# One layer of a hybrid diffusion backbone on one core: where the result is normalised, and three orders on three engines

## The reference

```python
h_lat = modulate(rms_norm(x, norm_g[l, 0]), mod_lat[0], mod_lat[1])     # h_ctx alike
m_ctx, m_lat = hybrid_mixer(h_ctx, h_lat, ...)      # gated DeltaNet heads and Mamba-2 heads, both directions
x = x + mod_lat[2] * rms_norm(m_lat, norm_g[l, 1])
h_lat = modulate(rms_norm(x, norm_g[l, 2]), mod_lat[3], mod_lat[4])
y_lat = ec_moe(h_lat, router_w[l], exp_w_gate[l], exp_w_up[l], exp_w_down[l])
x = x + mod_lat[5] * rms_norm(y_lat, norm_g[l, 3])
```

```python
gate, idx = lax.top_k(jnp.swapaxes(aff, 1, 2), cap)                # cap = 128
hid = silu(xs @ w_gate) * (xs @ w_up)
ye = (hid @ w_down) * gate[..., None]
y = zeros.at[bidx, idx].add(ye)                                    # a token may have several experts, or none
```

## Time and profile before

| what | us |
| --- | --- |
| median of 3 runs | 1538.88 (1536.69 to 1540.21) |
| the profiled execution | 1535.95 |
| its span, first to last instruction | 1534.1 |
| TensorE (PE) busy | 1312.0, 86% |
| VectorE (DVE) busy | 763.1, 50% |
| ScalarE (ACT) busy | 476.5, 31% |
| GpSimd (POOL) busy | 210.5, 14% |

### The profile page before, as it was taken

How to read it: one execution, slowest core, us unless ns; L and a number is a source line. 1 busy time by engine, 2 the same in 40 slices (tenths; PEclk the granted TensorE clock), 3 DMA queues, 4 the chain that set the end, 5 groups by cost and what they waited for, 6 DMA issues and landing times.

```text
span 1534.1 us, 13869 instructions
## 1 busy us (share of the span) xinstructions
PE 1312.0 (86%) x5053; PEld 759.5 (50%) x5053; DVE 763.1 (50%) x1080; ACT 476.5 (31%) x1109; POOL 210.5 (14%) x186
## 2 busy tenths in 40 slices
PE   6898889993999999988899978999239999999990
PEld 1444445441554555578888864455114444444440
DVE  1248878788760666637777764554640100110015
ACT  1625434351111122346666642333101010101003
POOL 0003210120100000015444410000010101110100
PEclk9899999997899999989999988999559999999995
DMA  8514343343142110035665572341729999999836
GB/s 307 154 28 147 112 144 117 103 122 100 69 138 82 42 27 28 9 96 158 184 186 181 179 272 98 136 150 56 265 78 334 341 341 328 333 339 342 282 83 232
DMA packets 173402, 257.81 MB, mean 168 GB/s; under 512 B 48861, under 2 KB 91606, under 8 KB 173334
## 3 DMA queue, kind: packets, MB, share of 16 engines
q1 hardware_dynamic: 152438, 208.52, 40.6%
q0 software_dynamic: 11392, 41.95, 9.2%
q10 hardware_dynamic: 9504, 6.45, 1.3%
HBM read 212.38 MB, written 44.50 MB: 167 GB/s over the span
## 4 chain that ended last, share of the span: by engine, by line
PE 68%; DVE 13%; ACT 10%; DMA 5%; issue 2%; SPq 2%; ACTq 0%; POOLq 0%; DVEq 0%
PE ps L1600 27%; PE ps L1056 15%; PE ps L1075 7%; PE ps L375 5%; DMA arena<-zt_dram 2%; PE ps L1020 2%; DVE arena L648 2%; PE ps L1558 2%; PE ps L458 2%; DVE arena L1961 1%; PE ps L1582 1%; ACT arena L1736 1%; PE ps L1045 1%; ACT arena L512 1%; DMA arena<-ada_w 1%
## 5 line engine op out<-in xcount | busy, mean ns | idle before, releaser
L1600 PE MATMUL ps<-arena 128*128 128x512 f32 (+1 forms) x1120 | 444.8, 557 | 0.0
L1600 PEld LDWEIGHTS ps<-arena 128*128 128x128 f32 x1120 | 214.0, 193 | 217.7 <-issue 212.3
L1056 PE MATMUL ps<-arena 128*128 128x512 f32 x512 | 227.9, 598 | 1.4 <-ACT arena L1172 1.4
L1961 DVE SCALAR_TENSOR_TENSOR arena<-arena,taps 128x1024 f32<-128x1024 f32 x160 | 223.5, 1397 | 5.7
L375 PE MATMUL ps<-arena 128*128 128x128 f32 x1080 | 136.5, 282 | 26.5 <-DVE arena L602 16.4
L1056 PEld LDWEIGHTS ps<-arena 128*128 128x128 f32 x512 | 96.9, 192 | 117.5 <-issue 115.5
L375 PEld LDWEIGHTS ps<-arena 128*128 128x128 f32 x1080 | 130.4, 197 | 35.9 <-issue 24.5
L1315 DVE TENSOR_TENSOR arena<-arena,ps 128x512 f32<-128x512 f32 x16 | 11.0, 688 | 226.5 <-PE ps L1056 226.5
L1020 PE MATMUL ps<-arena 128*128 128x512 f32 x256 | 116.2, 609 | 4.6 <-ACT arena L1121 4.6
L1075 PE MATMUL ps<-arena 128*128 128x512 f32 x256 | 112.6, 593 | 1.2 <-DVE arena L1322 1.2
L1020 PEld LDWEIGHTS ps<-arena 128*128 128x128 f32 x256 | 48.5, 194 | 62.9 <-issue 56.2
(11 more groups left out here) (280 smaller groups left out, 1593.4 us busy)
## 6 DMA issues: line engine op xcount, KB each, us to landing
arena<-exp_w_gate SPq DMA_DIRECT2D x16, 2048.0 KB, 11.2
arena<-exp_w_up SPq DMA_DIRECT2D x16, 2048.0 KB, 9.2
arena<-exp_w_down SPq DMA_DIRECT2D x16, 2048.0 KB, 11.0
arena<-ada_w POOLq DMA_DIRECT2D x16, 1024.0 KB, 6.2
arena<-w_in SPq DMA_DIRECT2D x28, 512.0 KB, 3.9
arena<-ada_w SPq DMA_DIRECT2D x4, 2048.0 KB, 10.6
arena<-x SPq DMA_DIRECT2D x16, 512.0 KB, 9.4
arena<-g_dram SPq DMA_DIRECT2D x16, 512.0 KB, 4.7
```

Source lines behind the costliest of these rows:

```text
L1056: last = mm(ps[gu_bank[s] + j][:], xsT[s][:, k, :], ew[s][j][:, k, :], start=(k == 0), stop=(k == KD - 1))
L1600: last = mm(ps[3 * (m % 2) + gi][:, 0:w], wring[(m + 1) % NW][:, k, :], hT[:, k, o:o + w], start=(k == 0), stop=(k == KD - 1))
L1961: ins = v.scalar_tensor_tensor(accg, cin_l[ci % 2][:, j // 3:j // 3 + GR, j % 3:j % 3 + GW], tp[:, j:j + 1], accg, ALU.mult, ALU.add)
```

## The change

There are five edits.

1. ScalarE's exponential of the blocks moves from the front of stage 12 to the end of stage 13.
2. On VectorE, `scores` moves from the end of an iteration (for `nxt`) to the next iteration, right behind `rest` (for `own`).
3. On GpSimd, `query_e` moves ahead of `with_eg` and `decayed_hs`.
4. GpSimd also stores each tile of x2 to `out` during the merge.
5. The end is rebuilt. `y_dram` is loaded once the first 14 experts' scatters have landed, into the memory of x2. Six of its tiles are normalised beside the products of experts 14 and 15, two behind them, and GpSimd adds each to `out` by an accumulating DMA. The rows of the tokens of experts 14 and 15 are then redone: their y rows are gathered, the expert's own result is added, they are normalised again, x2's rows (gathered from `out` earlier) are added, and the rows overwrite those in `out`. Expert 14's result is still scattered into `y_dram`, since 15 may share its tokens; expert 15's is not.

```diff
# 1 (scalar)
-                if m == M_Z0:
+                take_tile(m)
+                take_jobs(m)
+                if m == M_Z0 + 1:
                     act.wait_ge(sem("blk_dve"), 1)
                     a(yo_f, yo_f, ACT.Exp).then_inc(sem("blk_exp"), 1)
-                take_tile(m)
-                take_jobs(m)
# 2 (dve_scan)
                 if own and own[1] > 0:
                     rest(own)
+                if lat(own):
+                    scores(own)
                 if own and two:
                     mask_dn(dve, two)
...
                 if nxt:
                     block_y(nxt)
-                if lat(nxt):
-                    scores(nxt)
# 3 (pool_scan)
+                if lat(nxt):
+                    query_e(nxt)
                 if nxt and nxt[1] > 0:
                     with_eg(nxt)
                 if own and 0 < own[1] < LAST:
                     decayed_hs(own)
-                if lat(nxt):
-                    query_e(nxt)
# 4 (pool_tail, merge)
                 pool.dma_start(h2_t[ORD[t]], h2[t % 2]).then_inc(sem(f"h2_out{t % 2}"), 16)
+                pool.dma_start(out_t[ORD[t]], x2[:, ORD[t], :]).then_inc(sem("x2_out"), 16)
# 5 sp_tail
-            sp_.wait_ge(sem("y_sc"), 16 * E_N)
-            sp_.wait_ge(sem("down"), E_N)
+            sp_.wait_ge(sem("y_sc"), 16 * EL)
+            sp_.wait_ge(sem("x2_out"), 16 * NL)
             for t in range(NL):
                 sp_.dma_start(yt[:, t, :], y_t[t]).then_inc(sem(f"tile_in{t // 2}"), 16)
...
# 5 act_tail: six roots ahead of the copy of expert 15's hidT, two behind it, then those of the rows
             for e in range(E_N + 1):
+                if e == E_N:
+                    for t in range(N_FIRST):
+                        tile_root(t)
...
+            for t in range(N_FIRST, NL):
+                tile_root(t)
+            for i in range(LE):
+                act.wait_ge(sem("rows"), i + 1)
+                root_of(NL + i, yr[i])
# 5 dve_tail
             for e in range(E_N + 1):
+                if e == E_N - 1:
+                    for t in range(3):
+                        scaled(t, yt[:, t, :]).then_inc(sem("fin"), 1)
...                                                  # the hidden product of e
+                if e == E_N - 1:
+                    for t in range(3, N_FIRST):
+                        scaled(t, yt[:, t, :]).then_inc(sem("fin"), 1)
-                if e >= 1:
+                if 1 <= e < E_N:
...                                                  # ye of e - 1
+            dve.wait_ge(sem("ye"), E_N - 1)
+            dve.wait_ge(sem(f"xs_in{EL % NX}"), 16 * (E_N // NX + 1))
+            v.tensor_tensor(yr[0], yr[0], ye[EL % 2], ALU.add).then_inc(sem("rows"), 1)
+            for t in range(N_FIRST, NL):
+                scaled(t, yt[:, t, :]).then_inc(sem("fin"), 1)
+            dve.wait_ge(sem("down"), E_N)
+            dve.wait_ge(sem(f"xs_in{EL % NX + 1}"), 16 * (E_N // NX + 1))
+            for h in range(2):
...
+                ins = v.scalar_tensor_tensor(yr[1][:, hs_], ps[4 + h][:], gateT[:, E_N - 1:E_N], yr[1][:, hs_], ALU.mult, ALU.add)
+            ins.then_inc(sem("rows"), 1)
+            for i in range(LE):
+                link(scaled(NL + i, yr[i]))
+                dve.wait_ge(sem(f"xs_in{EL % NX - 2 + i}"), 16 * (E_N // NX + 1))
+                v.tensor_tensor(yr[i], yr[i], x2r[i], ALU.add).then_inc(sem("fin"), 1)
# 5 pool_tail
+            def added(t):
+                pool.wait_ge(sem("fin"), t + 1)
+                pool.dma_start(out_t[t], yt[:, t, :], accum_op=ALU.add).then_inc(sem("out"), 16)
-            for e in range(E_N):
+            for e in range(E_N - 1):
...
+                if e == EL - 1:
+                    pool.wait_ge(sem("x2_out"), 16 * NL)
+                    for i in range(LE):
+                        rows_in(x2r[i], out_rows, EL + i, EL % NX - 2 + i)
+                if e == EL:
+                    pool.wait_ge(sem("y_sc"), 16 * e)
+                    rows_in(yr[0], y_dram, EL, EL % NX)
+                    for i in range(NL // 2):
+                        pool.wait_ge(sem(f"tile_in{i}"), 64)
+                    for i in range(3):
+                        pool.wait_ge(sem(f"xs_in{i}"), 16 * (E_N // NX + 1))
+                    for t in range(N_FIRST):
+                        added(t)
...                                                  # wait for ye of e, scatter it
+            pool.wait_ge(sem("y_sc"), 16 * (E_N - 1))
+            rows_in(yr[1], y_dram, E_N - 1, EL % NX + 1)
+            for t in range(N_FIRST, NL):
+                added(t)
+            pool.wait_ge(sem("out"), 16 * NL)
+            for i in range(LE):
+                pool.wait_ge(sem("fin"), NL + i + 1)
+                if i > 0:
+                    pool.wait_ge(sem("out_rows"), 16 * i)
+                p.indirect_dma_start(out_rows, ...idxT of expert EL + i..., yr[i], None).then_inc(sem("out_rows"), 16)
```

More of the change, by code:

```diff
@@ L886, in hybrid_block @@
         gu_bank = (2, 6)
-        yt = arena[:, 0:NL * D].rearrange("p (t n) -> p t n", t=NL)
+        LE = 2
+        EL = E_N - LE
+        yt = x2
+        x2r, yr = (xs[EL % NX - 2], xs[EL % NX - 1]), (xs[EL % NX], xs[EL % NX + 1])
+        assert NX == 4 and EL % NX == 2
+        N_FIRST = 6
         wo_k = w_out.rearrange("a (k p) n -> (a p) k n", p=P)
@@ L895, in hybrid_block @@
         out_t = out.rearrange("a (t p) d -> (a t) p d", p=P)
+        out_rows = out.rearrange("a t d -> (a t) d")
         ORD = [NL // 2 - 1 - t // 2 if t % 2 == 0 else NL // 2 + t // 2 for t in range(NL)]
@@ L959, in sp_tail @@
                 load_down(e)
-            sp_.wait_ge(sem("y_sc"), 16 * E_N)
-            sp_.wait_ge(sem("down"), E_N)
+            sp_.wait_ge(sem("y_sc"), 16 * EL)
+            sp_.wait_ge(sem("x2_out"), 16 * NL)
             for t in range(NL):
                 sp_.dma_start(yt[:, t, :], y_t[t]).then_inc(sem(f"tile_in{t // 2}"), 16)
-            for t in range(NL):
-                sp_.wait_ge(sem("fin"), t + 1)
-                sp_.dma_start(out_t[t], yt[:, t, :]).then_inc(sem("out"), 16)
             sp_.wait_ge(sem("out"), 16 * NL)
+            sp_.wait_ge(sem("out_rows"), 16 * LE)
         def pe_tail(pe):
@@ L1172, in xs_copy, with root_of, tile_root @@
                 a(xsT[e % 2][:, 4 * h:4 * h + 4, :], heads(ps[0][:]), ACT.Copy).then_inc(sem("xsT"), 1)
+            def root_of(i, src):
+                a(sqj, src, ACT.Square, accum_out=ssq[:, i:i + 1]).then_inc(sem("ysq"), 1)
+                act.wait_ge(sem("ysq"), 2 * i + 1)
+                a(rstd[:, i:i + 1], ssq[:, i:i + 1], ACT.Sqrt, scale=1.0 / D, bias=eps1[:]).then_inc(sem("ysq"), 1)
+            def tile_root(t):
+                act.wait_ge(sem(f"tile_in{t // 2}"), 64)
+                root_of(t, yt[:, t, :])
             xs_copy(0, 0)
@@ L1309, in dve_tail, with scaled @@
             dve.wait_ge(sem("route"), 5)
+            def scaled(i, src):
+                dve.wait_ge(sem("ysq"), 2 * i + 2)
+                link(v.reciprocal(rstd[:, i:i + 1], rstd[:, i:i + 1]))
+                return v.scalar_tensor_tensor(src, src, rstd[:, i:i + 1], row5, ALU.mult, ALU.mult)
             for e in range(E_N + 1):
+                if e == E_N - 1:
+                    for t in range(3):
+                        scaled(t, yt[:, t, :]).then_inc(sem("fin"), 1)
                 if e < E_N:
@@ L1322, in dve_tail @@
                     v.tensor_scalar(ye[s][:, 512:D], ps[5][:], gateT[:, e - 1:e], None, ALU.mult).then_inc(sem("ye"), 1)
[L1323 to L1327, removed]
+            dve.wait_ge(sem("ye"), E_N - 1)
[6 more added lines that the diff above has]
+            for h in range(2):
+                hs_ = slice(h * 512, (h + 1) * 512)
+                ins = v.scalar_tensor_tensor(yr[1][:, hs_], ps[4 + h][:], gateT[:, E_N - 1:E_N], yr[1][:, hs_], ALU.mult, ALU.add)
[4 more added lines that the diff above has]
+                v.tensor_tensor(yr[i], yr[i], x2r[i], ALU.add).then_inc(sem("fin"), 1)
         def pool_tail(pool):
@@ L1345, in pool_tail, with rows_in @@
                 gather(e)
-            for e in range(E_N):
+            def rows_in(dst, src, e, k):
+                pool.wait_ge(sem("xsps"), 2 * (E_N - NX + k + 1))
+                p.indirect_dma_start(dst, None, src, bass.IndirectOffsetOnAxis(ap=idxT[:, e:e + 1], axis=0))\
+                    .then_inc(sem(f"xs_in{k}"), 16)
+            def added(t):
+                pool.wait_ge(sem("fin"), t + 1)
+                pool.dma_start(out_t[t], yt[:, t, :], accum_op=ALU.add).then_inc(sem("out"), 16)
+            for e in range(E_N - 1):
                 if 1 <= e <= E_N - NX:
```

2 lines of the change are left out of this document (added).

## The result

The changed kernel takes 1504.17 us, the median of 4 runs (1503.4 to 1504.98), and the kernel before took 1537.87 beside it: a ratio of 0.9779, interval 0.9762 to 0.9796. The forecast was 1495.5 with a range of 1482 to 1510. The sign and the range held; the point is 8.7 us too low. In the profiled execution (1504.78, span 1502.9) the gain is 31.2 us of span where the sum had 43.4.

| landmark | before | after | moved | forecast |
| --- | --- | --- | --- | --- |
| tile 13 evacuated | 404.92 | 377.72 | -27.2 | -29.1 |
| first V convolution | 506.80 | 481.30 | -25.5 | -28.8 |
| first latent residual (L602) | 709.27 | 680.56 | -28.7 | |
| last residual | 900.33 | 867.22 | -33.1 | |
| w_out loaded, the merge | 909.25 | 879.43 | -29.8 | -37.4 |

The account below looks back on a forecast made before the run. TensorE was taken to carry most of the chain, with three stretches in which it waits or is over. Terms -29.1 - 8.3 + 1 - 7.0 = -43.4 gave 1495.5 us, against a median of 1538.88; range 1482 to 1510.

Parts of the forecast that it names:

- The exponential: Projection: ScalarE no longer waits before the exponential, so tile 13 is evacuated earlier; -29.1 us, bounds -27 and -30.
- The scan: Scan: with scores behind the residual subtraction a step goes from 12.74 to 12.4 us; together -8.3, bounds -2.3 and -15.
- the ring: Scan: ScalarE evacuations, SyncE's store, the decay-row load behind it, the mask and VectorE's scalings set the step, 12.4 us.
- Rival C: Scan: the step is not 12.4; 12.74 holds (1501.5 us) or it is 11.9 (1489); chance 0.18 for both sides.
- The -1.7 at the last step: Last latent scan step: the subtraction and the solve without its block product leave the chain; -1.7 us.
- query_e: GpSimd in the scan: kgT products and state decay start 1 to 2.5 us later, users come over 8 later; no effect.
- x2's stores: Merge: eight more 512 KB DMAs behind the h2 stores, mostly too late to disturb the zt load; +1 us, bounds 0 and +7.8.
- The tail: Rebuilt end: GpSimd's queue with nine accumulating DMAs at 2.65 us each sets the end; -7.0 us.
- Rival A: Tail: accumulating stores cost what the lone scatter does, 3.5 us; tail +0.8, total 1503.3 us; chance 0.21.
- B: Tail: accumulating stores cost little more than plain ones; tail -17, total 1485.5 us; chance 0.13.
- D: Tail: accumulating stores of one queue don't overlap, each takes 9.3 us; 60 us more, total 1555; chance 0.03.
- E: Projection: the exponential's edit gives half, as tile 12's jobs or late job hold TensorE; total 1510 us; chance 0.03.

Follow-up runs that it names:

- exp_alone: The kernel before with only the exponential moved, to behind tile 13 and its jobs: 1509.27 us, ratio 0.9814.
- store_behind: query_back with SyncE's store of the scan's output behind the load of the next decay rows: 1489.43 us, 0.9684 of the kernel before.
- query_back: The changed kernel with query_e on GpSimd back where it was before: 1498.64 us, 0.9736 of the kernel before.
- old_end: The kernel before with the exponential and the scores moved, no x2 stores and the old end: 1499.74 us, ratio 0.9757.
- scores_alone: The kernel before with only the scores moved behind the residual subtraction: 1528.52 us, ratio 0.9922.
- query_kept: both_orders with query_e ahead of with_eg on GpSimd: 1487.95 us, 0.9665 of the kernel before.
- query_alone: The kernel before with only query_e moved ahead of with_eg on GpSimd: 1538.62 us over 10 runs, ratio 1.0017.
- pool_waits: The kernel before with one more wait at GpSimd's very end, for all output stores: 1541.13 us over 12 runs, ratio 1.0018.
- both_orders: query_back with SyncE's scan store behind the next loads and expert 14's scatter behind the second tile store: 1485.16 us, 0.9649 of the kernel before.

## Why the prediction was right, and where it fell short

**The exponential: right in mechanism, some 0.5 to 2 us too much.** ScalarE's idle time, TensorE's gap, the cover on VectorE and the new place of the selects came as worked out, and exp_alone's -28.6 stands beside -29.1. In the trace tile 13 is 1.9 us late: TensorE's clock fell behind the late job's products of one column, while the forecast took its 19.14 us from a stage in which it had not fallen. The first V convolution is 3.3 us late against the forecast, but 1.7 of them are a second fall, behind the job of stage 14, which the profiled execution of the kernel before happened not to have and three other traces of that order do. Luck of one execution is no cost of the edit.

**The scan: the ring was right, the sum too large.** The step is 12.44 us against a forecast of 12.4, and the chain goes through the ring named. Rival C falls: neither 12.74 nor 11.9 is what the changed kernel does. (The 12.84 from which TensorE's 11.8 was worked out stands in no row; with the mean step it is 12.74 - 1.05 = 11.69, and store_behind, where TensorE's chain is 99%, has 11.68.) From the first V convolution to w_out exp_alone takes 400.8 us and query_back 394.9, so the edit is worth 6 there where 8.3 were forecast (8.8 by the ratios of exp_alone and old_end, 12.0 by that of scores_alone). The -1.7 at the last step did not come: from the last residual to w_out it takes 8.9 us before and 9.2 in query_back.

**query_e: "Nothing" was wrong.** This is the step whose mechanism failed; in us the tail missed more. The forecast saw that kgT comes later and asked only who multiplies with it. SyncE waits for the last kgT too, at the head of the merge, and behind that wait stand the merge's first loads. From the last residual to w_out it costs 3.3 us against the kernel before and 3.0 against query_back, and the ratios of the two give 6.6 in all. In query_kept it is 1.8 in the trace and 2.8 by the medians, and in query_alone nothing: the price depends on how late the loads are (4.0, 6.3 and 8.8 us ahead of the last residual). Why the steps of query_alone took 13.1 us was not settled: GpSimd waits 95.4 us for the query rows there (L703), where before it waited some 80 for the decay rows, and no run separates the two.

**x2's stores: +1 forecast, 0 to 1 by the traces.** By the rule that was weighed there (the Trainium skill, DMA: Bandwidth & Descriptors, "Issuing engines are not separate DMA queues") the price would have leaned to +7.8. The traces show the zt loads between 6.2 and 7.0 us, before between 6.1 and 6.9, the five on the chain 33.1 us in sum against 32.0, and 0.2 us for the merge. Merges of the same code differ by more than that from trace to trace (170.8 to 174.3 us with the stores, 170.0 to 173.2 without), so that the forecast's 1 us is neither shown nor excluded; 7.8 is excluded. The rule may hold for the engines they run on; most of the added bytes came when the load that counts was over. Behind the landing of the third zt load at 968.91 the engines still moved some 0.5 MB, the size of one store (414 GB/s from 969 to 970, 94 in the next us); before, behind the landing at 999.60, some 0.15.

**The tail: rate right, -7.0 forecast, -1.05 measured.** Moved by the 30.2 us that it started earlier, each step up to the scatter can be checked: first square 1449.9 forecast and 1450.07 measured, first accumulating store 1460.0 and 1459.95, down 1463.8 and 1463.40. An accumulating DMA was taken at 2.65 us and took 2.52. Rival A (3.5 us each, 1503.3) names nearly the time that was measured, and is wrong: its mechanism is not in the trace. What was missing are two terms. The first is 3.1 us up to the last landing (1499.9, where 1496.8 was forecast). The scatter lands 1.9 us late (1480.95 against 1479.1), though each DMA was cheaper than taken: the pipe fills slowly, with 61 GB/s from 1460 to 1463. The last pair of stores lands 3.1 us late (1491.3 against 1488.2): hardly anything moves from 1480.6 to 1483 (10 GB/s) while the gather and the stores are issued behind the scatter's landing, and the pair lands 9.1 us after its issue. The forecast's 1518.4 comes out as 1508.8 + 4.3 + 2 x 2.65: it started the gather when the scatter's bytes were through, with no landing and no issue in between. The row stores add nothing to the miss. The second is the closing, 3.0 us behind the last landing; the sum had taken none, as if the old end's 0.4 were nothing and the new one equal. pool_waits and the rows of the drains show that it belongs to GpSimd being last. Together they are the 6 us that the tail missed.

**The sum.** By ratios: the exponential -28.6, the scores -8.8, x2's stores and the end -3.2 (interval as wide as the value; 0 by the traces), query_e +6.6: -34.0, against a measured 1537.87 - 1504.17 = 33.7. That the two agree shows little: the four pieces are differences along one row of kernels (before, exp_alone, old_end, query_back, changed), and their sum is the last ratio whatever each of them is. The range held because two errors, in the scan and in the tail, were each inside its bounds, not because either was foreseen. Rivals B and D are refuted by 2.52 us for a DMA, E by exp_alone.

## What to carry to other kernels

When an operation is moved back in an in-order queue, list every engine that waits on its semaphore, the one that only issues DMAs among them: the user that counted here was a wait at the head of the next stage. When a ring of waits passes through a DMA queue, look at what is issued just ahead of the load in it; a store placed behind it took 0.7 us out of each of 15 steps, which was more than the rebuilt end was worth. And when the last work moves to another engine, price its closing and each landing that the next issue must wait for: a chain of DMAs costs its latencies, and only a row of them costs its rate.

## What the runs showed of the hardware

- Accumulating DMAs to DRAM in a row ran at 206 to 212 GB/s with all 16 engines full, half of the 410 of plain ones; GpSimd needed 0.9 us to issue one and 0.53 for a plain one.
- The end of the program took 2.7 to 3.6 us at its closing line where GpSimd came last (the changed kernel, both_orders, pool_waits), and 0.2 where it did not. GpSimd's drain there took 3.4 us with nothing under way (pool_waits), and 6.35 from beside its last DMA issue in the changed kernel; SyncE's took 0.007.
- TensorE's granted clock can fall while the engine is busy, here about 1 us behind 16 products of one column: 1.00 from 361 to 363 and 0.51, near 1.2 GHz, from 363 to 366, at the cost of 1.8 us for the 32 products that follow (15.68 instead of 13.90). The same stage has it in one execution and not in the next: behind the late job of stage 14 the products took 15.68 us in the changed kernel and in scores_alone, and 13.98 in the profile of the kernel before and in store_behind, as they did behind the late job at 245.73. That the products of one column are the cause is not shown.
